# Turning the gated values of a mixture of experts in 32 by 32 blocks on VectorE, with the down product in 22 full row blocks, and differential scores two units ahead

## What is computed

```python
def _swiglu(h, w1, w3, w2):
    return (jax.nn.silu(h @ w1) * (h @ w3)) @ w2

def _moe_swiglu(h, router_w, router_b, w1, w3, w2):
    ...
    out = jnp.zeros_like(h)
    for e in range(N_EXPERTS):
        out = out + gates[..., e:e + 1] * _swiglu(h, w1[e], w3[e], w2[e])
    return out
```

```python
def diff_attend(q, k, v, lam):
    s = jnp.einsum('bqhcd,bkhcd->bhcqk', q, k).astype(jnp.float32) * (DIFF_QK_DIM ** -0.5)
    p = jax.nn.softmax(s, axis=-1)
    pd = (p[:, :, 0] - lam * p[:, :, 1]).astype(v.dtype)
    return jnp.einsum('bhqk,bkhd->bqhd', pd, v)
```

## Time and profile before

| what | us |
|---|---|
| median of 3 runs | 3294.95 |
| lowest and highest | 3294.92, 3304.92 |
| the profiled execution | 3293.41 |
| its span, first to last instruction | 3291.6 |
| busy in the span: PE | 3116.3 |
| busy in the span: DVE | 1283.0 |
| busy in the span: ACT | 588.3 |

### The profile page before, as it was taken

One profiled execution on the slowest core, in us unless ns is written; L12 is line 12 of the kernel. 1 busy time (PEld: TensorE's weight loads), 2 busy tenths in 40 slices (PEclk: granted clock), 3 DMA queues, 4 the chain that ended last, 5 costly groups with the idle time before them and its releaser, 6 DMA issues.

```text
span 3291.6 us, 52527 instructions
## 1 busy us (share of the span) xinstructions
PE 3116.3 (95%) x22488; PEld 2069.7 (63%) x22488; DVE 1283.0 (39%) x2836; ACT 588.3 (18%) x1314; POOL 0.2 (0%) x4
## 2 busy tenths in 40 slices
PE   7999899999999999999999999999999879988998
PEld 5454799997344443457745555445557568876887
DVE  1568666666799887503410101000112232122211
ACT  2114222222211111203310110010111220012000
POOL 0000000000000000000000000000000000000000
PEclk8999999999999999999999999999999889999999
DMA  7241001001577886330189999999984114531452
GB/s 264 75 154 51 1 1 40 1 1 39 189 239 243 245 248 187 123 99 25 70 317 362 357 339 337 343 362 367 349 231 130 51 52 141 153 115 51 133 148 64
DMA packets 351595, 551.15 MB, mean 167 GB/s; under 512 B 14512, under 2 KB 292400, under 8 KB 348048
## 3 DMA queue, kind: packets, MB, share of 16 engines
q1 hardware_dynamic: 351376, 547.89, 50.2%
HBM read 546.80 MB, written 1.05 MB: 166 GB/s over the span
## 4 chain that ended last, share of the span: by engine, by line
PE 89%; DVE 6%; ACT 2%; DMA 2%; issue 1%; SPq 0%; DVEq 0%; ACTq 0%
PE bank L666 15%; PE bank L1337 14%; PE bank L928 9%; PE bank L1130 8%; PE bank L1359 8%; PE bank L1517 7%; PE bank L1144 3%; PE bank L631 3%; PE bank L745 3%; PE bank L1171 2%; PE bank L1075 2%; DVE mix L2079 2%; PE bank L912 1%; PE bank L1282 1%; DMA arena<-in_ada_w 1%; PE bank L1426 1%
## 5 line engine op out<-in xcount | busy, mean ns | idle before, releaser
L666 PE MATMUL bank<-a,ring 128*128 128x256 f32 (+1 forms) x1792 | 454.8, 417 | 19.0 <-ACT a L1614 12.0
L666 PEld LDWEIGHTS bank<-a,ring 128*128 128x128 f32 x1792 | 344.9, 193 | 126.5 <-issue 74.5
L2079 DVE SCALAR_TENSOR_TENSOR mix<-arena,csil,mix 128x256 f32<-128x256 f32 x1008 | 402.0, 476 | 45.6 <-ACT mix L1618 45.6
L1337 PE MATMUL bank<-ring,arena 128*32 128x352 f32 x5376 | 406.9, 461 | 2.7 <-ACT small L1876 2.7
L1337 PEld LDWEIGHTS bank<-ring,arena 128*32 128x32 f32 x5376 | 175.1, 110 | 221.4 <-issue 220.4
L1130 PE MATMUL bank<-a,ring 128*128 128x512 f32 x704 | 307.5, 596 | 6.8 <-ACT a L1614 6.8
L1130 PEld LDWEIGHTS bank<-a,ring 128*128 128x128 f32 x704 | 133.2, 191 | 179.7 <-issue 178.0
L1517 PE MATMUL bank<-arena,ring 128*128 128x256 f32 x1024 | 223.5, 379 | 1.9 <-DVE arena L2736 1.9
L1618 ACT ACTIVATE arena<-bank 128x256 f32<-128x256 f32 (+1 forms) x303 | 142.0, 473 | 451.7 <-PE bank L928 199.2
L2638 DVE TENSOR_TENSOR arena<-arena,bank 128x352 f32<-128x352 f32 x48 | 25.0, 521 | 501.3 <-ACT arena L1889 501.3
L1359 PE MATMUL bank<-ring,arena 128*32 128x256 f32 (+1 forms) x3840 | 219.0, 380 | 0.6 <-issue 0.6
(11 more groups left out here) (411 smaller groups left out, 3360.6 us busy)
## 6 DMA issues: line engine op xcount, KB each, us to landing
ring<-in_moe_w SPq DMA_DIRECT2D x224, 704.0 KB, 8.4
ring<-in_mlp_w SPq DMA_DIRECT2D x64, 1024.0 KB, 5.5
ring<-in_moe_w SPq DMA_DIRECT2D x112, 512.0 KB, 8.4
arena<-in_ada_w SPq DMA_DIRECT2D x96, 512.0 KB, 3.8
arena<-in_w_ada SPq DMA_DIRECT2D x48, 512.0 KB, 3.6
ring<-in_ffn_w SPq DMA_DIRECT2D x22, 1024.0 KB, 8.5
arena<-in_moe_w SPq DMA_DIRECT2D x32, 704.0 KB, 8.8
ring<-in_moe_w SPq DMA_DIRECT2D x48, 384.0 KB, 8.4
```

Of the source, the lines that this page charges most:

```text
L666: i = mm(bank[b][:, 0:n], ws[:, k, t * P:t * P + P], rhs[:, k, sl], start=(k == 0), stop=(k == KT - 1))
L1337: i = mm(b[32 * t:32 * t + 32, 0:PART], ac_[:, k, 32 * g:32 * g + 32], ws[i_][:, PART * t:PART * t + PART], start=(k == 0), stop=(k == KT ...
L2079: ins = V.scalar_tensor_tensor(dst, x, cond, dst, ALU.mult, ALU.add)
```

## The change

In the experts the three PE transposes of each half and group and the two ACT copies behind them are gone, TURN_BANKS with them. In their place DVE turns hid into gT with one instruction of 128 x 352 that turns each block of 32 by 32 by itself. Column block c of gT then holds, on its 128 partitions, units 32c to 32c+31 of each of the four parts t, so that the down product goes over 11 column blocks for each half (DOWN), 22 items of 128 rows instead of 24 of 128 or 96. The rows of w2 for such an item lie in four runs of 32 rows, 352 rows apart, and the DMA's source is written with that shape. A block has 54 items; the slots are no longer used equally often, and uses(i) counts that. In the attention PE takes the scores of unit w+2 where it took those of w+1.

```diff
-PIECES = ((0, 128), (128, 128), (256, 96))
-BLOCKS_AT = [(p, t, i) for p in range(2) for t in range(4) for i in range(3)]
-ITEMS = 32 + len(BLOCKS_AT)
+DOWN = [(p, c) for p in range(2) for c in range(PART // 32)]
+ITEMS = 32 + len(DOWN)
+def uses(i):
+    return len(range(i % MRING, ITEMS, MRING))
...
-                            prev = (i - MRING) % ITEMS
+                            prev = i - MRING if i >= MRING else i + MRING * (uses(i) - 1)
...
-                                p, t, piece = BLOCKS_AT[i - 32]
-                                o, n = PIECES[piece]
-                                f0 = MCOLS * p + PART * t + o
-                                src = w["moe_w2"][0][one, f0:f0 + n, :]
-                                dst = dst[0:n, 0:D]
-                            src = src.rearrange("e p n -> p (e n)")
+                                p, c = DOWN[i - 32]
+                                src = w["moe_w2"][0][one, MCOLS * p:MCOLS * p + MCOLS, :]
+                                src = src.rearrange("e (t r) n -> (e t) r n", t=4)[:, 32 * c:32 * c + 32, :]
+                                dst = dst[:, 0:D]
+                            if i < 32:
+                                src = src.rearrange("e p n -> p (e n)")
...
-                        if p == 1 and k in (2, 3, 4):
-                            if k == 2:
-                                of_vec(("hid", 0, 2))
-                            if k == 4:
-                                of_act(("gT", 0, 0))
-                            hidden_turned(0, k - 2)
-                for n, (p, t, piece) in enumerate(BLOCKS_AT):
-                    o, rows_ = PIECES[piece]
+                for n, (p, c) in enumerate(DOWN):
                     ws = landed(32 + n)
                     for g in range(GROUPS_OF):
-                        if n == 0:
+                        if n == 0 and g == 0:
+                            of_vec(("gT", 0, 2))
                             of_vec(("hid", 1, 0))
-                        if n % 12 == 0:
-                            of_act(("gT", p, g))
+                        if c == 0 and p == 1:
+                            of_vec(("gT", 1, g))
                         for q in range(4):
                             i = mm(bank[Y_BANKS[g]][32 * q:32 * q + 32, 0:256],
-                                   gT[0:rows_, p, g, o + 32 * t:o + 32 * t + 32],
-                                   ws[0:rows_, 256 * q:256 * q + 256], start=(n == 0),
-                                   stop=(n == len(BLOCKS_AT) - 1), skip_group_check=True)
+                                   gT[:, p, g, 32 * c:32 * c + 32],
+                                   ws[:, 256 * q:256 * q + 256], start=(n == 0),
+                                   stop=(n == len(DOWN) - 1), skip_group_check=True)
...
             scores2(0)
+            scores2(1)
             for w_ in range(len(DIFF_UNITS)):
-                if w_ + 1 < len(DIFF_UNITS):
-                    scores2(w_ + 1)
+                if w_ + 2 < len(DIFF_UNITS):
+                    scores2(w_ + 2)
...
-                    for g in range(GROUPS_OF):
-                        of_pe(("turned", p, g))
-                        b = bank[TURN_BANKS[p][g]]
-                        act(gT[:, p, g, 0:256], b[:, 0:256], ACT.Copy).then_inc(ac_moe, did(ACM, ("gT part", p, g)))
-                        act(gT[0:96, p, g, 256:384], b[0:96, 256:384], ACT.Copy
-                            ).then_inc(ac_moe, did(ACM, ("gT", p, g)))
...
+                def hidden_turned(p, g):
+
+                    ve.wait_ge(ve_moe, e * per + at(VEM, ("hid", p, g)))
+                    V.transpose(gT[:, p, g, :], hid[:, p, g, :]).then_inc(ve_moe, did(VEM, ("gT", p, g)))
...
                                         ).then_inc(ve_moe, did(VEM, ("hid", p, g)))
+                        if g:
+                            hidden_turned(p, g - 1)
+                    hidden_turned(p, GROUPS_OF - 1)
```

More of the change, by code:

```diff
@@ L424, in build @@
         hid = cut(arena, 768, 2, GROUPS_OF, PART)
-        gT = cut(arena, 2880, 2, GROUPS_OF, 3 * P)
+        gT = cut(arena, 2880, 2, GROUPS_OF, PART)
         yp, pgt = cut(arena, 5184, GROUPS_OF, 256), cut(arena, 5952, GROUPS_OF, 256)
@@ L432, in build @@
         UP_BANKS = ((0, 1, 2, 3, 4, 5), (6, 7, 0, 1, 2, 3))
-        TURN_BANKS = ((4, 5, 4), (4, 0, 1))
         Y_BANKS = (6, 7, 5)
@@ L1313, in landed @@
                 def landed(i):
-                    pe.wait_ge(m_full[i % MRING], e * (16 * (ITEMS // MRING)) + 16 * (i // MRING + 1))
+                    pe.wait_ge(m_full[i % MRING], e * (16 * uses(i)) + 16 * (i // MRING + 1))
                     return m_slots[i % MRING]
-                def hidden_turned(p, g):
-                    b = bank[TURN_BANKS[p][g]]
-                    for o, n in PIECES:
-                        i = nc.tensor.transpose(b[0:n, o:o + P], hid[:, p, g, o:o + n], ident)
-                    i.then_inc(pe_moe, mark(PEM, ("turned", p, g)))
                 for p in range(2):
@@ L1343, in expert_block @@
                             i.then_inc(pe_moe, mark(PEM, ("up", p, k)))
-                        if p == 1 and k in (2, 3, 4):
-                            if k == 2:
-                                of_vec(("hid", 0, 2))
-                            if k == 4:
-                                of_act(("gT", 0, 0))
-                            hidden_turned(0, k - 2)
-                for n, (p, t, piece) in enumerate(BLOCKS_AT):
-                    o, rows_ = PIECES[piece]
+                for n, (p, c) in enumerate(DOWN):
                     ws = landed(32 + n)
                     for g in range(GROUPS_OF):
-                        if n == 0:
+                        if n == 0 and g == 0:
+                            of_vec(("gT", 0, 2))
                             of_vec(("hid", 1, 0))
-                        if n % 12 == 0:
-                            of_act(("gT", p, g))
+                        if c == 0 and p == 1:
+                            of_vec(("gT", 1, g))
                         for q in range(4):
                             i = mm(bank[Y_BANKS[g]][32 * q:32 * q + 32, 0:256],
-                                   gT[0:rows_, p, g, o + 32 * t:o + 32 * t + 32],
-                                   ws[0:rows_, 256 * q:256 * q + 256], start=(n == 0),
-                                   stop=(n == len(BLOCKS_AT) - 1), skip_group_check=True)
+                                   gT[:, p, g, 32 * c:32 * c + 32],
+                                   ws[:, 256 * q:256 * q + 256], start=(n == 0),
+                                   stop=(n == len(DOWN) - 1), skip_group_check=True)
                     i.then_inc(pe_moe, mark(PEM, ("down", n)))
[L1364 to L1368, removed]
                     if n == 7:
                         of_vec(("hid", 1, 2))
-                        of_act(("gT", 1, 2))
                         of_act_last(("y", 2))
@@ L1901, in _ @@
                 gathered("gathered", ac_moe, ACM)
-                of_pe(("down", len(BLOCKS_AT) - 1))
+                of_pe(("down", len(DOWN) - 1))
                 for g in range(GROUPS_OF):
```

## The result

| | median us | runs | lowest to highest |
|---|---|---|---|
| before | 3294.93 | 4 | 3294.56 to 3304.92 |
| changed kernel | 3846.80 | 4 | 3844.15 to 3850.17 |

The ratio is 1.1667, 95% interval 1.1642 to 1.1691. The forecast was 3816, the range 3775 to 4120. The profiled execution of the changed kernel took 3844.15 us, its span is 3842.4.

The account below looks back on a forecast made before the run. The prediction took PE's own work to bound the kernel, with the DMA engines close behind in the experts. Experts +539 and attention -16 on the profiled 3293.41 us gave 3293.41 + 523 = 3816 us, range 3775 to 4120.

## What to carry to other kernels

Before changing what a DMA gathers, write down the outermost count of both access patterns: a source of 4 runs of 32 rows moves at about a quarter of the rate of 128 rows (105 against 395 GB/s), with the same bytes in packets of the same size. Where the rows must be permuted, permute the other operand in SBUF instead, in runs of some 32 columns, and keep them 8 bytes apart or less where there are no runs. And price a stretch whose waits go away at the clock that a PE without gaps is granted, not at the one that it has while it waits.

## What was new about the hardware

- Loads on four engines hold SP back once a few are queued. In the first block of the changed kernel the first five issues of w2 take 0.55 to 1.38 us, the sixth 8.72, and from there most take 4.6 (4.59 in the chain above), near the 4.99 at which the items land; in the kernel before, the first issues of w2 take 0.33 to 0.38. The fifth, sixth and seventh in the chain of the changed kernel:

```profile
1702.14 0.55 SPq L600
1702.88 8.72 SPq L600
...
1711.86 4.73 SPq L600
```

- Full engines do not mean a full rate: shares of 1.02 to 1.04 stand at 395 to 415 GB/s with 128-row loads, at 246 with 96-row loads among them, at 251 and 271 with 32-row loads, and at 242 with four-engine loads among sixteen-engine ones. A packet of 4 KB takes 168 ns on average in the window at 395, and 273, 265, 244 and 278 in the others. The Trainium skill, page "DMA: Bandwidth & Descriptors", section "The descriptor swizzle", says that in a transfer to 128 partitions each engine writes a port of its own. That the other shapes are slow because engines share ports would fit these rows, but no run here shows which engine wrote where, so it stays an argument.
- The moving operand of a fp32 matmul read 16 or 44 bytes apart costs 1.75 times the time, 8 bytes apart 1.03, in runs of 128 bytes 1.00.
